# Products of expert weights taken two groups and two u tiles at a time in a hybrid SSD, attention and PEER block

## What is computed

```python
sc = einsum('thjd,hjnd->thjn', q, sub_keys)      # 8 heads, 2 halves, 128 keys each
s_half, i_half = top_k(sc, 16)                   # then the best 16 of 16 x 16 pairs
idx = i_first * 128 + i_second                   # one of 16384 experts
g = softmax(top_s)
h = gelu(einsum('td,thkd->thk', xb, u[idx]))
out = einsum('thk,thkd->td', g * h, v[idx])      # 8 x 16 = 128 experts for each token
```

## Time and profile before

| | |
|---|---|
| median of three runs | 1400.7 us |
| profiled execution, span from first to last instruction | 1396.6 us |
| what lies around the span (median less span) | 4.1 us |
| TensorE busy | 1364.6 us, 98% |
| VectorE busy | 1083.6 us, 78% |
| ScalarE busy | 435.3 us, 31% |
| GpSimd busy | 610.1 us, 44% |
| moved by DMA | 467.69 MB, mean 335 GB/s |

### The profile page before, as it was taken

How to read it: one execution, slowest core, us unless ns; L and a number is a source line. 1 busy time by engine, 2 the same in 40 slices (tenths; PEclk the granted TensorE clock), 3 DMA queues, 4 the chain that set the end, 5 groups by cost and what they waited for, 6 DMA issues and landing times.

```text
span 1396.6 us, 16311 instructions
## 1 busy us (share of the span) xinstructions
PE 1364.6 (98%) x5402; PEld 933.1 (67%) x5402; DVE 1083.6 (78%) x2469; ACT 435.3 (31%) x1219; POOL 610.1 (44%) x516
## 2 busy tenths in 40 slices
PE   7999999999998999999999999999999999999998
PEld 5656648566587888888899999995444444444443
DVE  4535445899899999999999999998777677766656
ACT  2533532544411111112787887872000000000000
POOL 0000001733855444434466655664577645754440
PEclk9999999999999999999999999999999999999999
DMA  8322234975999999989899999999999999999997
GB/s 321 140 107 99 116 149 172 371 287 208 406 366 407 375 332 384 326 302 316 296 394 400 403 405 385 391 384 389 363 409 409 409 409 409 410 409 409 410 409 308
DMA packets 121763, 467.69 MB, mean 335 GB/s; under 512 B 13776, under 2 KB 14160, under 8 KB 115152
## 3 DMA queue, kind: packets, MB, share of 16 engines
q0 software_dynamic: 73728, 268.47, 49.9%
q1 hardware_dynamic: 47664, 197.66, 36.6%
q10 hardware_dynamic: 288, 0.52, 0.1%
HBM read 462.67 MB, written 3.93 MB: 334 GB/s over the span
## 4 chain that ended last, share of the span: by engine, by line
PE 60%; DMA 22%; DVE 9%; issue 3%; POOL 3%; ACT 2%; another core or an unknown queue 0%; DVEq 0%; SPq 0%; ACTq 0%; POOLq 0%
PE BANKS L929 32%; PE BANKS L729 11%; PE BANKS L721 9%; DMA BIG<-v,IDX 7%; DMA BIG<-u,IDX 7%; DMA UV<-v,IDX 4%; PE BANKS L948 4%; DMA UV<-u,IDX 2%; POOL BIG L1665 2%; DVE X L1623 1%; POOL UV L1665 1%; DVE BIG L1618 1%; DVE UV L1618 1%; DMA T<-away 1%; PE BANKS L912 1%
## 5 line engine op out<-in xcount | busy, mean ns | idle before, releaser
L1665 POOL DMA_INDIRECT UV<-u,IDX x153 | 184.1, 1203 | 411.1 <-DVE IDX L1495 263.3
L1665 POOL DMA_INDIRECT UV<-v,IDX x159 | 191.1, 1202 | 121.0 <-DVE X L1623 51.2
L1623 DVE SCALAR_TENSOR_TENSOR X<-UV,HG,X 128x1024 f32<-128x1024 f32 x159 | 203.9, 1282 | 40.7 <-DMA UV<-v,IDX 36.3
L929 PE MATMUL BANKS<-T 128*128 128x256 f32 x1024 | 229.2, 379 | 1.0 <-issue 1.0
L953 PE MATMUL BANKS<-T,BIG 128*128 128x512 f32 x512 | 225.2, 592 | 0.2 <-DMA T<-v 0.2
L953 PE MATMUL BANKS<-Y,BIG 128*128 128x512 f32 x512 | 225.1, 592 | 0.0
L929 PE MATMUL BANKS<-T,Y 128*128 128x256 f32 x992 | 221.9, 379 | 0.0
L1618 DVE SCALAR_TENSOR_TENSOR UV<-UV,Y 128x1024 f32<-128x1024 f32 x153 | 186.3, 1221 | 42.5 <-DMA UV<-u,IDX 37.7
L929 PEld LDWEIGHTS BANKS<-T 128*128 128x128 f32 x1024 | 192.0, 190 | 26.1 <-issue 1.4
L929 PEld LDWEIGHTS BANKS<-T,Y 128*128 128x128 f32 x992 | 186.0, 190 | 24.0
L953 PEld LDWEIGHTS BANKS<-Y,BIG 128*128 128x128 f32 x512 | 97.3, 190 | 122.5 <-issue 122.5
(11 more groups left out here) (272 smaller groups left out, 1243.6 us busy)
## 6 DMA issues: line engine op xcount, KB each, us to landing
T<-u_t SPq DMA_DIRECT2D x64, 512.0 KB
T<-v SPq DMA_DIRECT2D x64, 512.0 KB
Y<-v SPq DMA_DIRECT2D x64, 512.0 KB
Y<-u_t SPq DMA_DIRECT2D x62, 512.0 KB
BIG<-w_in SPq DMA_DIRECT2D x23, 1024.0 KB, 4.8
BIG<-w_q SPq DMA_DIRECT2D x16, 1024.0 KB, 6.9
BIG<-w_out SPq DMA_DIRECT2D x8, 1024.0 KB, 4.9
UV<-v,IDX POOLq DMA_INDIRECT x159
```

The source lines that it names most:

```text
L929: last = nc.tensor.matmul(PS[(i + 2) % 4][:, 0:HT], ub[:, c, :], T8[:, 1, c, :], start=(c == 0), stop=(c == KC - 1))
L1623: stt(xb, row, HG[:, n % 2, i % UNIT:i % UNIT + 1], xb, ALU.mult, ALU.add).then_inc(used, 1)
L1665: pool.indirect_dma_start(row_place(s), None, u if kind == "ru" else v, bass.IndirectOffsetOnAxis(IDX[:, b, c:c + 1], 0)).then_inc(row_in[ ...
```

## The change

The step list writes the second half of the u stage in pairs: "gm g" and "gw j" exist only for even g and j, and each does the work of two. The product takes the columns of groups g and g + 1 in one instruction, reading PSUM banks 4 + g % 4 and the next, four elements of the one and four of the other in turn (`by_group`, `group_banks`); ScalarE's copy does the same; "gw" takes two u tiles and two banks. The waits of TensorE and ScalarE count pairs. The rows between the steps are set anew, and the first "gm" stand ahead of u tile 68:

```diff
--- before.py
+++ after.py
@@ -210,20 +210,19 @@
             spent += cost[work[w][0]]
             w += 1
     o += work[w:]
-    g = 0
-    for k, j in enumerate(range(FIRSTJ, NKEY)):
-        if 0 < g < NGRP - 1:
-            o += on("oh", g + 1)
+    for j in range(FIRSTJ, NKEY, 2):
+        g = j - FIRSTJ
+        o += on("oh", g + 1) if g else []
         o += rows(1)
-        if k >= 3:
-            o += [("gm", n) for n in range(max(0, g - 3), g) if ("gm", n) not in o]
+        if g == 4:
+            o += on("gm", 0)
+        o += on("gm", g - 2) if g >= 4 else []
         o += on("gl", j) + on("og", g)
-        g += 1
-        if k == 2:
-            o += on("sel", 1)
-        o += on("gw", j - 1)
-        o += rows(1 + (k % 4 == 0))
-    o += on("gm", NGRP - 1) + on("gw", NKEY - 1)
+        o += on("gw", j - 2) + rows(1)
+        o += on("sel", 1) if g == 2 else []
+        o += on("oh", g + 2) if g + 2 < NGRP else []
+        o += rows(1) + on("gl", j + 1) + on("og", g + 1) + rows(1 + (g % 4 != 2))
+    o += on("gm", NGRP - 2) + on("gw", NKEY - 2)
     first, second, keys, columns = pick(LATE)
     o += rows(2) + [first] + rows(2) + [second] + rows(1) + [keys] + rows(1) + [columns]
     for n in range(LATE + 1, NUNIT):
@@ -416,9 +415,9 @@
                 done[0] += 1
             elif step == "gm":
                 JS[i] = done[0]
-                done[1] += 1
-        WEIGHED = {j: n for n, j in enumerate(j for j in range(NKEY) if KW[j])}
-        COPIED = {g: n for n, g in enumerate(g for g in range(NGRP) if JS[g] < NKEY)}
+                done[1] += 2
+        WEIGHED = {j: n for n, j in enumerate(j for j in range(0, NKEY, 2) if KW[j])}
+        COPIED = {g: n for n, g in enumerate(g for g in range(0, NGRP, 2) if JS[g] < NKEY)}
         kind_of = lambda n: 2 if n >= NUNIT else int(n >= LATE)
         CHOSEN = nth(("r",))
         EXPS = nth(("e",))
@@ -427,7 +426,7 @@
 
         POS = {s: i for i, s in enumerate(ORDER)}
         rows_until = lambda step: sum(s[0] in ("ru", "rv") for s in ORDER[:POS[step]])
-        FIRST_V = rows_until(("gm", NGRP - 1))
+        FIRST_V = rows_until(("gm", NGRP - 2))
 
         def spaces():
 
@@ -497,6 +496,13 @@
 
         def abs_count(g):
             return sum(NTOK - ACT_FROM[i % 2] for i in range(g))
+
+        def by_group(g, first, end):
+
+            return HBUF[:, first:end, g * NTOK:(g + 2) * NTOK].rearrange("p j (a t) -> p j a t", t=NTOK)
+
+        def group_banks(g, first, end):
+            return BANKS[:, 4 + g % 4:6 + g % 4, :].rearrange("p a (j t) -> p j a t", t=NTOK)[:, first:end]
 
         def y_count(kind, b):
             return 1 + NORMS[("NF"[kind - 1], b)]
@@ -923,7 +929,7 @@
                     if i >= 4:
                         pe.wait_ge(ge_done, i - 3)
                         if KW[i - 4]:
-                            pe.wait_ge(gw_done, WEIGHED[i - 4] + 1)
+                            pe.wait_ge(gw_done, WEIGHED[(i - 4) // 2 * 2] + 1)
                     ub = u_place(i).rearrange("p (c i) -> p c i", i=NKEY)
                     for c in range(KC):
                         last = nc.tensor.matmul(PS[(i + 2) % 4][:, 0:HT], ub[:, c, :], T8[:, 1, c, :],
@@ -940,9 +946,9 @@
                     if i in (0, 3):
                         pe.wait_ge(selt_done, 4 if i else 2)
                     if i >= 4:
-                        pe.wait_ge(gm_done, i - 3)
-                        if i - 4 in COPIED:
-                            pe.wait_ge(gc_done, COPIED[i - 4] + 1)
+                        pe.wait_ge(gm_done, (i - 4) // 2 + 1)
+                        if (i - 4) // 2 * 2 in COPIED:
+                            pe.wait_ge(gc_done, COPIED[(i - 4) // 2 * 2] + 1)
                     bank = PS[4 + i % 4][:, :].rearrange("p (j t) -> p j t", t=NTOK)
                     for k in range(NTOK):
                         last = nc.tensor.matmul(bank[:, :, k], ONEHOT[:, i % 2, 0, k, :], ONEHOT[:, i % 2, 1, k, :],
@@ -959,12 +965,12 @@
                     last = v_half(j, t, n)
                 return last
 
-            pe.wait_ge(gm_done, NGRP - 2)
+            pe.wait_ge(gm_done, NGRP // 2 - 1)
             pe.wait_ge(gc_done, sum(g < NGRP - 2 for g in COPIED))
             for j in range(3):
                 pe.wait_ge(v_in[j], 16)
                 v_products(j, 0)
-            pe.wait_ge(gm_done, NGRP)
+            pe.wait_ge(gm_done, NGRP // 2)
             pe.wait_ge(gc_done, len(COPIED))
             for j in range(3):
                 v_products(j, 1).then_inc(vd_full, 1)
@@ -1201,10 +1207,9 @@
                         act.wait_ge(idx_ready, LATE)
                         act.wait_ge(selt_done, 2 * HB)
                         act.wait_ge(used, CLOSED[FIRSTJ] + 1)
-                    act.wait_ge(gm_done, i + 1)
-                    nc.scalar.activation(HBUF[:, JS[i]:NKEY, i * NTOK:(i + 1) * NTOK],
-                                         PS[4 + i % 4].rearrange("p (j t) -> p j t", t=NTOK)[:, JS[i]:NKEY, :],
-                                         ACT.Copy).then_inc(gc_done, 1)
+                    act.wait_ge(gm_done, i // 2 + 1)
+                    nc.scalar.activation(by_group(i, JS[i], NKEY), group_banks(i, JS[i], NKEY), ACT.Copy)\
+                        .then_inc(gc_done, 1)
                 elif step == "sel":
                     act.wait_ge(selt_full, i + 1)
                     act.wait_ge(dense_keys, len(DENSE))
@@ -1633,14 +1638,14 @@
                 elif step == "oh":
                     onehots(i)
                 elif step == "gm":
-                    dve.wait_ge(gb_full, i + 1)
+                    dve.wait_ge(gb_full, i + 2)
                     dve.wait_ge(ge_done, JS[i])
-                    hb = HBUF[:, 0:JS[i], i * NTOK:(i + 1) * NTOK]
-                    tt(hb, hb, PS[4 + i % 4].rearrange("p (j t) -> p j t", t=NTOK)[:, 0:JS[i], :], ALU.mult)\
-                        .then_inc(gm_done, 1)
+                    hb = by_group(i, 0, JS[i])
+                    tt(hb, hb, group_banks(i, 0, JS[i]), ALU.mult).then_inc(gm_done, 1)
                 elif step == "gw" and KW[i]:
-                    dve.wait_ge(ge_done, i + 1)
-                    tt(HBUF[:, i, 0:KW[i]], HBUF[:, i, 0:KW[i]], PS[(i + 2) % 4][:, 0:KW[i]], ALU.mult).then_inc(gw_done, 1)
+                    dve.wait_ge(ge_done, i + 2)
+                    hb = HBUF[:, i:i + 2, 0:KW[i]]
+                    tt(hb, hb, BANKS[:, (i + 2) % 4:(i + 2) % 4 + 2, 0:KW[i]], ALU.mult).then_inc(gw_done, 1)
                 elif step == "fin":
                     dve.wait_ge(x_back, 16)
                     for n in range(2):
```

## The result

| | before | after |
|---|---|---|
| median | 1400.9 us (15 runs) | 1407.9 us (15 runs) |
| ratio after / before, 95% interval | | 1.0048 (1.0035 to 1.0061) |
| span of the profiled execution | 1396.6 us | 1402.3 us |

The median rose by 7.1 us where 3.6 us were forecast. The profiled execution of after took 1404.1 us, so 1.8 us lie around its span, not the 4.1 us that I assumed. If the same holds for before (an estimate: 1396.6 + 1.8 = 1398.4 us), its profile is of an execution some 2.3 us under that kernel's median. The profile of after is further off still: it is the fastest of the 15 runs, 3.8 us under their median. What follows is therefore read from two quick executions, which differ by 5.7 us of span.

What follows compares the result with a forecast made beforehand. TensorE, fed without a gap, was taken to bound the stage. Span 1396.6 + 4.0 (late first product) - 0.4 (tail) = 1400.2 us, timed 1404.3 us; range 1402.5 to 1405.6 us (0.68), with A and B 1399.8 to 1407.0 us (0.85).

Steps and rivals of the forecast that it cites:

- the 4.1 us: Outside the profiled span: 1400.7 us median less 1396.6 us span, assumed unchanged and added to the forecast span.
- Step (3): Start of the pairs: the late first product makes TensorE's group 4 start 4.0 us late, range 3.8 to 4.9 us.
- Step (4): Rest of the paired u stage: 6 us or more of room for banks and one-hots, no wait follows; 0 us.
- Step (1): Second half of the u stage: 63 fewer instructions save 4 us of VectorE, hidden behind TensorE; 0 us of span.
- Step (2): Row steps of the paired stage: 144 before and after, so no sixteen extra rows; 0 us.
- D: Rival: the row count is wrong and 16 more rows are done in this stage; timed 1402.7 us, chance 0.01.
- Rival B: The pause at group 4 also lowers TensorE's clock, about 2.0 us more; 1406.3 us, 1407.2 with the long pause; chance 0.12.
- Step (5): End of the kernel: rows are pushed less than TensorE, saving 0.4 of at most 2.0 us of the additions.
- C: Rival: products reading two PSUM banks cost more per element, 1413 us at double cost; chance 0.05.
- A: Rival: no pause at group 4, since VectorE reaches the first products early enough; 1399.5 to 1401.2 us, chance 0.12.
- E: Rival: the kernel gets faster by over 0.5%, needing TensorE to lose idle time it doesn't have; chance 0.02.

Runs made afterwards that it cites:

- e15: e1 unchanged, in a second profiled execution; TensorE lost 4.5 us between groups 3 and 63.
- e1: The changed kernel with its first two paired group products moved directly behind group 3; 1.0026 of the kernel before.
- e9: e6 with six gathered rows more among groups 2 to 22; 1.0089 of the kernel before.
- e12: The kernel before with six gathered rows more among groups 2 to 22; 1.0062 of the kernel before.
- e3: The kernel before, nothing paired, with its first three group products one step later; 1.0022 of the kernel before.
- e6: e1 with the u tile products single again, group products and copies still paired; 1.0022 of the kernel before.
- e4: The changed kernel with its first two paired group products behind the one-hot of group 5, ahead of ru 108 and weights 2; 1.0052 of the kernel before.
- e13: e1 with six gathered rows fewer among groups 4 to 44, done after group 63 instead; 1.0044 of the kernel before.
- e10: e1's list with every product single, standing two by two where the pairs stood; 1.0041 of the kernel before.
- e14: The kernel before, unchanged, in a second profiled execution; TensorE lost 2.7 us between groups 3 and 63, span 1402.0 us.
- e7: e1 with the paired u tile product ahead of the paired group product; 1.0022 of the kernel before.
- e8: e1 with three rows fewer in groups 4 to 12; 1.0022 of the kernel before.

## Why the prediction was wrong

**What failed.** Two terms of the sum. Step (3) priced the late first product at 4.0 us of pause and nothing for the clock; the profile of after has 5.58 and 2.24 us, a loss of 7.8 us. Step (4) put the steady state at nothing; without the pause the paired list loses 4.5 and 4.8 us (e15, e1) and its runs are 1.0026 of the kernel before, some 3.6 us. That is about what the forecast of 3.6 us lacks to the measured 7.1. By how much each term is to blame in a typical run of after stays open: its one profile shows only the first, the ratios give each about half.

**Step (1), fewer instructions: right in kind.** 63 fewer, 3.4 us less of VectorE's busy time against my 4 us, and hidden.

**Step (2), no sixteen rows: right** by the count, and D is out: with six rows more the loss grew by 12 us or more (e9, e12), not the 7.8 of after.

**Step (3), the first product late: right place, undersized.** One wait, at group 4, released by ScalarE's copy, as said. I took 4.0 us from a range of 3.8 to 4.9; it was 5.58. Group 4 started at 697.28 us, not 696.4, 0.9 us more, nearly all of it because rv 62 waited 2.73 us for its row and the product came at 695.73 instead of 695.0; and TensorE was 0.72 us earlier at group 3, so it stood for longer. 4.0 + 0.9 + 0.7 = 5.6 us. My bounds took VectorE's arrival and TensorE's as fixed at one profile's values, and TensorE's alone varies by 4 us over the profiles.

**Rival B, the clock: it happened, and it was held to be unlikely (0.12).** Its price of 2.0 us was good: 2.24 us in after, 1.75 in e3. The argument against it was the 3.6 us pause near 430 us at full clock. That was the exception: a second execution of the same kernel lost its clock at that very pause, and the clock fell at that place in 14 of the 17 profiles. The Trainium skill (TensorE: Matmul & The Clock Gate, "Why this matters for your kernels") advises no idle gaps over about 3 us. The pauses of 5.4, 5.3 and 3.4 us at group 4 agree, and near 430 us all pauses of 3.4 to 3.6 us but the first profile of before; but pauses of 2.0 us at group 4 (e6) and 2.1 us near 430 us (after) lowered the clock as well. B's 1407.2 us is 0.7 us from the median, which is partly luck: B had the clock but not the small losses of the steady state. The range stopped at 1407.0, under B's own upper figure.

**Step (4), the steady state: failed.** "6 us or more of room" and no wait: in the profile of after indeed none shows. But without the pause (e1, e15) the paired list loses 4.5 to 4.8 us, and in e4, with it, 3.4 us. I looked at engines and buffers and took from one profile without a wait that there was slack. e12 and e13 show that the number of rows in the stage decides. It also fits the sizes of the medians: after is 7.1 us over before, e1 3.9; taking away a pause of 5.6 + 2.2 us gave only about 3 us.

**Step (5), the tail: roughly right.** 1.0 us came back between the last matmul and the end of the span (6.7 against 5.7 us) where I took 0.4 of at most 2.0.

**The 4.1 us around the span: wrong as a length, harmless in the sum.** In after they were 1.8 us; the rest is, by that estimate, a profile below its median. The term only puts the forecast on top of the median of before, which is where it belongs. In the trace, span to span, the forecast of +3.6 met +5.7 us; the medians' +7.1 us is more, and no second profile of after shows why.

**C is out.** 1,008 elements in 1.20 us, against 0.67 us for 504: elements of alternating banks cost what those of one bank do. A and E are out as well: the pause is there, and the kernel isn't faster.

**Open.** Whether the list of e1 is slower than the kernel before by its pairs or by its order: e10, with the order and without pairs, is no faster by its ratio of 1.0041, and that is larger than its profile's loss of 2.5 us explains. The lists of e1 and e15 read at 385 and 386 GB/s against 395 and 388 (before, e14), which may be cause or effect. And whether the transfers or the five places of the ring hold up the rows.

## What to carry to other kernels

When TensorE is busy for the whole of a stage and the DMA share is at 1 as well, another limit may be near, and here all 14 changed kernels came out slower than the kernel before: before such a change, move a few transfers in and out of the stage and see which way the time goes. A first consumer that moves one step later delays what waits for it, and the clock can fall behind the pause. And take two profiles of the kernel before, and set each profiled run beside the median of its kernel: a margin of half a microsecond, or a pause that didn't cost the clock, read from one execution is not yet a property of the kernel.

## What the runs showed that was not expected

- After pauses of 2.0 to 5.4 us at group 4 the next group and u tile took 1.8 to 2.2 us longer, the granted clock at 0.50 for some 4 us in after (after, e3, e4, e6); after pauses of 1.8 and 1.7 us they didn't (e7, e8). Near 430 us the same matmuls ran behind a pause in all 17 profiles, at a lower clock in 14, and a pause of 3.6 us lowered it in e12 and e13 and not in the first profile of before.
- In the profile of e12 one more row of 512 KB cost 2.6 us of loss (15.8 us for six), though its bytes take 1.3 us at 395 GB/s and VectorE's work on it 1.28 us; by the ratio it was some 1.5 us a row.
- A product that reads two PSUM banks in turn, four elements each, runs at the speed of one bank (1.20 us for 1,008 elements).
